# Forming the turns of an S5 layer earlier: where sixteen angle and sine blocks stand in a fused two-layer kernel

## The reference, cut to what matters

```python
q_dn, kv_dn, k_rope, gate = jnp.split(h @ w_in, MLA_SPLITS, axis=-1)
```

```python
lam_dt = lam * dt[:, None]
powers = jnp.exp(lam_dt[None] * jnp.arange(1, S5_CHUNK + 1, dtype=jnp.float32)[:, None, None])
```

## Time and profile before

| | us |
|---|---|
| median of three executions | 1883.57 |
| lowest and highest | 1883.27, 1885.47 |
| profiled execution, its own time | 1888.0 |
| its span in the trace | 1886.2 |

### The profile page before, as it was taken

How to read it: one execution, slowest core, us unless ns; L and a number is a source line. 1 busy time by engine, 2 the same in 40 slices (tenths; PEclk the granted TensorE clock), 3 DMA queues, 4 the chain that set the end, 5 groups by cost and what they waited for, 6 DMA issues and landing times.

```text
span 1886.2 us, 27230 instructions
## 1 busy us (share of the span) xinstructions
PE 1646.9 (87%) x10616; PEld 1230.7 (65%) x10616; DVE 659.5 (35%) x1225; ACT 409.9 (22%) x922; POOL 661.3 (35%) x678
## 2 busy tenths in 40 slices
PE   3899659999999959999566699999989998999997
PEld 3444225555554438888455588888878786888786
DVE  4565936565550042230666600001023012233301
ACT  1303333323220020001544410000021001244300
POOL 0026999999899999600333200000000000000000
PEclk9999879999999989999877799999999999999999
DMA  8669878788788866326898854444423432344431
GB/s 268 192 200 250 219 167 173 173 184 205 195 193 194 192 139 148 111 67 228 253 300 280 239 160 148 154 156 133 156 77 125 134 112 67 121 148 154 150 124 61
DMA packets 241230, 318.31 MB, mean 169 GB/s; under 512 B 32274, under 2 KB 211061, under 8 KB 236405
## 3 DMA queue, kind: packets, MB, share of 16 engines
q1 hardware_dynamic: 204736, 227.58, 37.8%
q0 software_dynamic: 33072, 80.79, 20.1%
q10 hardware_dynamic: 3333, 8.71, 1.4%
HBM read 258.28 MB, written 50.33 MB: 164 GB/s over the span
## 4 chain that ended last, share of the span: by engine, by line
PE 75%; DVE 8%; DMA 5%; ACT 4%; issue 4%; SPq 3%; DVEq 0%; ACTq 0%; PEldq 0%
PE bank L830 34%; PE bank L1143 12%; PE bank L1028 6%; DMA arena<-s_b_powers 3%; PE bank L897 2%; SPq L646 2%; DMA s_turns<-arena 2%; PE bank L854 2%; PE bank L1083 1%; PE bank L1199 1%; PE bank L961 1%; PE bank L930 1%; PE bank L929 1%; PE bank L927 1%; PE bank L928 1%
## 5 line engine op out<-in xcount | busy, mean ns | idle before, releaser
L830 PE MATMUL bank<-ht,ring 128*128 128x256 f32 (+1 forms) x1664 | 425.9, 419 | 27.0 <-ACT gate L1344 16.4
L830 PEld LDWEIGHTS bank<-ht,ring 128*128 128x128 f32 x1664 | 321.9, 194 | 128.8 <-issue 89.3
L1143 PE MATMUL bank<-arena,ring 128*128 128x256 f32 x1024 | 223.2, 381 | 1.0 <-PEq L1134 1.0
L1143 PEld LDWEIGHTS bank<-arena,ring 128*128 128x128 f32 x1024 | 195.9, 191 | 28.1 <-issue 1.2
L830 PE MATMUL bank<-gate,ring 128*128 128x256 f32 (+1 forms) x640 | 195.0, 467 | 4.9 <-DVE gate L2176 3.4
L830 PEld LDWEIGHTS bank<-gate,ring 128*128 128x128 f32 x640 | 122.6, 192 | 76.8 <-issue 63.1
L1028 PE MATMUL bank<-ring,ht 128*128 128x256 f32 x512 | 116.5, 391 | 17.4 <-DVE ht L1777 17.4
L1028 PEld LDWEIGHTS bank<-ring,ht 128*128 128x128 f32 x512 | 100.5, 197 | 32.1 <-issue 17.8
L830 PE MATMUL bank<-arena,ring 128*128 128x256 f32 x480 | 108.0, 388 | 3.9 <-DVE arena L2238 3.9
L830 PEld LDWEIGHTS bank<-arena,ring 128*128 128x128 f32 x480 | 93.8, 196 | 17.9 <-DVE arena L2238 4.3
L2375 POOL DMA_DIRECT2D arena<-arena x128 | 64.7, 513 | 109.9 <-ACT arena L1505 108.0
(11 more groups left out here) (362 smaller groups left out, 2349.4 us busy)
## 6 DMA issues: line engine op xcount, KB each, us to landing
ring<-in_s_w_glu SPq DMA_DIRECT2D x32, 1024.0 KB, 5.3
ring<-in_w_mod SPq DMA_DIRECT2D x24, 1024.0 KB, 9.1
ring<-in_w_up SPq DMA_DIRECT2D x22, 1024.0 KB, 5.1
arena<-s_b_rows POOLq DMA_DIRECT2D x32, 512.0 KB, 11.6
arena<-s_power_rows POOLq DMA_DIRECT2D x32, 512.0 KB, 11.6
s_b_powers<-arena POOLq DMA_DIRECT2D x32, 512.0 KB, 3.1
s_c_powers<-arena POOLq DMA_DIRECT2D x32, 512.0 KB, 5.6
ring<-in_s_w_in SPq DMA_DIRECT2D x16, 1024.0 KB, 5.5
```

Source lines behind the costliest of these rows:

```text
L830: mm = pe.matmul(psum[2 * (u % 2) + m][:, 0:mv.free_size()], ring[:, sl, k, m * P:(m + 1) * P], mv, start=(kg == 0 and k == 0), stop=(kg = ...
L1143: mm = pe.matmul(psum[4 * par + 2 * (s // 2) + m][:, 0:S], ring[:, sl, k, m * P:(m + 1) * P], yt[:, kg * 8 + k, :], start=(kg == 0 and k = ...
```

## The change

Six of the sixteen blocks (0 to 5) are formed during the MLA head, angle and sines both. Angles 0 and 1 stand on DVE ahead of the copies of `qd`, angles 2 to 5 behind them, and ACT takes the six blocks ahead of its squares. Two more output buffers are laid over free room at the start of the arena, so the first four blocks have a buffer each; blocks 4 and 5 go back to the first two and wait for stores. Angles 6 to 9 are also formed there, and kept in four extra buffers in the same room, so DVE first waits until all six stores have landed. ACT may write the second half of `b_and_c` (that is `ccol`, which lies over the angle and output buffers) only after angle 9 is formed and the six stores have landed. The other blocks stand behind gate units 2 (6, 7, 8), 3 (9, 10, 11), 4 (12, 13) and 5 (14, 15). DVE forms angles 10 to 15 ahead of the normalisation of queries and keys, and none behind it. The wait of ACT for `bc_spilled` moves from unit 4 to unit 2. No operation is added or taken away.

```diff
+        trig_angle += [carve(512 * i, 2, BLK, NC5) for i in range(4)]
+        trig_out += [carve(1024 * i, 2, 2, BLK, NC5) for i in range(2)]
+        def angle_of(b):
+            return trig_angle[b - 4 if 6 <= b < 10 else b % 2]
+        def trig_of(b):
+            return trig_out[b if b < 4 else b % 2]
...
             def b_and_c():
                 for f in range(16):
+                    if f == 8:
+                        act.wait_ge(ang_set, 10)
+                        for par in range(2):
+                            act.wait_ge(trig_stored[par], 16 * 3)
...
             modulate(0)
+            def trig(b):
+                par = b % 2
+                angle, o = angle_of(b), trig_of(b)
+                act.wait_ge(ang_set, b + 1)
+                if b >= 4:
+                    act.wait_ge(trig_stored[par], 16 * (b // 2))
...
+            for b in range(6):
+                trig(b)
...
-            trigs = ((), (), (0, 1, 2), (3, 4, 5), (6, 7, 8, 9), (10, 11, 12, 13), (14, 15), ())
+            trigs = ((), (), (6, 7, 8), (9, 10, 11), (12, 13), (14, 15), (), ())
             for s in range(8):
                 if s == 4:
...
-                    act.wait_ge(bc_spilled, 8 * 16)
-                gate_silu(s)
+                gate_silu(s)
+                if s == 2:
+                    act.wait_ge(bc_spilled, 8 * 16)
...
+            def angles(b):
+                angle = angle_of(b)
+                if 2 <= b < 6 or b >= 10:
+                    dve.wait_ge(trig_set, 2 * (b - 6 if b in (10, 11) else b - 2) + 2)
...
+            for b in range(2):
+                angles(b)
             dve.wait_ge(par_got, 6)
...
+            for b in range(2, 6):
+                angles(b)
             dve.wait_ge(slot_done, at + 2)
...
+            for par in range(2):
+                dve.wait_ge(trig_stored[par], 16 * 3)
+            for b in range(6, 10):
+                angles(b)
...
-            for b in range(6):
+            for b in range(10, NB5):
                 angles(b)
             dve.wait_ge(root_set, 2)
...
-            for b in range(6, NB5):
-                angles(b)
```

More of the change, by code:

```diff
@@ L1332, in _ @@
             modulate(0)
+            def trig(b):
[4 more added lines that the diff above has]
+                    act.wait_ge(trig_stored[par], 16 * (b // 2))
+                act.activation(o[:, 1], angle, ACT.Sin, scale=-TWO_PI_DOWN).then_inc(trig_set, 1)
+                link(act.activation(o[:, 0], angle, ACT.Abs))
+                act.activation(o[:, 0], o[:, 0], ACT.Sin, scale=-TWO_PI_DOWN, bias=half_pi).then_inc(trig_set, 1)
+                act.wait_ge(trig_set, 2 * b + 2)
+                act.dma_start(spill_trig[b], o.rearrange("p z d q c -> p (z d q c)")).then_inc(trig_stored[par], 16)
+            for b in range(6):
+                trig(b)
             for j in range(2):
@@ L1345, in gate_silu @@
                         .then_inc(unit_free[(u0 + s) % 2], 1)
-            def trig(b):
-                par = b % 2
-                act.wait_ge(ang_set, b + 1)
-                if b >= 2:
-                    act.wait_ge(trig_stored[par], 16 * (b // 2))
-                act.activation(trig_out[par][:, 1], trig_angle[par], ACT.Sin, scale=-TWO_PI_DOWN).then_inc(trig_set, 1)
-                link(act.activation(trig_out[par][:, 0], trig_angle[par], ACT.Abs))
-                act.activation(trig_out[par][:, 0], trig_out[par][:, 0], ACT.Sin, scale=-TWO_PI_DOWN, bias=half_pi)\
-                    .then_inc(trig_set, 1)
-                act.wait_ge(trig_set, 2 * b + 2)
-                act.dma_start(spill_trig[b], trig_out[par].rearrange("p z d q c -> p (z d q c)")).then_inc(trig_stored[par], 16)
-            trigs = ((), (), (0, 1, 2), (3, 4, 5), (6, 7, 8, 9), (10, 11, 12, 13), (14, 15), ())
+            trigs = ((), (), (6, 7, 8), (9, 10, 11), (12, 13), (14, 15), (), ())
             for s in range(8):
@@ L1819, in _ @@
                 dve.tensor_copy(pw[:, z, :, GP5:P], pn[:, z, ::-1, GP5:P]).then_inc(par_got, 1)
+            def angles(b):
+                angle = angle_of(b)
+                if 2 <= b < 6 or b >= 10:
+                    dve.wait_ge(trig_set, 2 * (b - 6 if b in (10, 11) else b - 2) + 2)
+                ph = phi[:, :].rearrange("p (d q) -> p d q", d=2)[:, :, b * BLK:(b + 1) * BLK].unsqueeze(3).to_broadcast(wide)
+                link(tt(angle, ph, iota.unsqueeze(1).unsqueeze(1).to_broadcast(wide), ALU.mult))
+                link(ts(trig_near, angle, MAGIC, None, ALU.add))
+                stt(out=angle, in0=trig_near, scalar=-MAGIC, in1=angle, op0=ALU.add, op1=ALU.subtract).then_inc(ang_set, 1)
+                dve.wait_ge(ang_set, b + 1)
+            for b in range(2):
+                angles(b)
             dve.wait_ge(par_got, 6)
@@ L1863, in _ @@
             dve.wait_ge(bc_spilled, 8 * 16)
-            def angles(b):
-                par = b % 2
-                if b >= 2:
-                    dve.wait_ge(trig_set, 2 * b - 2)
-                ph = phi[:, :].rearrange("p (d q) -> p d q", d=2)[:, :, b * BLK:(b + 1) * BLK].unsqueeze(3).to_broadcast(wide)
-                link(tt(trig_angle[par], ph, iota.unsqueeze(1).unsqueeze(1).to_broadcast(wide), ALU.mult))
-                link(ts(trig_near, trig_angle[par], MAGIC, None, ALU.add))
-                stt(out=trig_angle[par], in0=trig_near, scalar=-MAGIC, in1=trig_angle[par], op0=ALU.add, op1=ALU.subtract)\
-                    .then_inc(ang_set, 1)
-                dve.wait_ge(ang_set, b + 1)
-            for b in range(6):
+            for b in range(10, NB5):
                 angles(b)
```

## The result

| kernel | median us (lowest to highest, executions) | ratio to before, 95% |
|---|---|---|
| before | 1883.42 (1881.20 to 1885.47, 4) | |
| changed | 1853.45 (1852.55 to 1855.85, 4) | 0.9836 (0.9811 to 0.9862) |
| changed, second time | 1854.56 (1851.23 to 1858.36, 4) | 0.9849 (0.9827 to 0.9871) |
| changed, third time | 1853.54 (1849.20 to 1857.27, 4) | 0.9837 (0.9814 to 0.9859) |

The change makes the kernel 30.0 us faster, where 36.8 was forecast. The time lies in the range (1842 to 1859) and 6.7 us above the forecast of 1846.8. The changed kernel's profiled execution took 1855.85 us, with a span of 1854.0 where before had 1886.2.

What follows compares the result with a forecast made beforehand. PE was taken to bound the kernel, with two waits for ACT totalling 38.9 us. Heads 34.8 us earlier, net of a 5.7 us head delay, plus 1.95 for their first products gave 36.8 us, so 1846.8 us; range 1842 to 1859.

Steps and rivals of the forecast that it cites:

- Both gaps: PE's waits for ACT around gate unit 7, 16.4 us before it and 22.5 before the heads; both would go.
- third rival: Gate units: silu 4 comes out behind 191.9 and PE waits again, 2 to 8 us each, 1849 to 1855; 5%.
- POOL's tables (fourth): S5 layer: POOL's tables bind its start and the kernel is slower, 1889 us or up to 1905; 3%.
- the normalisation (first): Before the heads: DVE's normalisation, behind angle 15, becomes last; 0 to 8 us, 1847 to 1855; upper part 20%.
- the forecast's own upper bound without rivals: Whole kernel: 1851 us, if the two store landings in the head sum to 13 us.
- A: Head: landing time of the store of block 2, which block 4 waits for; taken as 3.5 us.
- B: Head: landing time of the store of block 5, which DVE waits for beside a 1 MB gate load; 5 us.
- A + B - 2.8: Head: delay of the second half of `b_and_c` from two store landings; 5.7 us, bounds 2.4 to 21.2.
- The clock was charged at nothing: Head: PE's clock stays full if PE goes on with turning pieces; no charge, otherwise about 2 to 3 us.
- 221.2: Start of the heads in us, instead of 256.02, with both gaps gone and unit 7 at full clock; 34.8 us saved.
- Against the median, to which the same saving applies: Whole kernel: the 36.8 us summed from the profiled execution also come off the median 1883.57, giving 1846.8.
- Nothing else of the later stages changes: Behind the heads: the 36.8 us stand to the end; POOL's table slack falls from 89.4 to 46.9 us.

Runs made afterwards that it cites:

- head only: Changed kernel with blocks 6 to 15 back where they stood before, six blocks and ten angles still in the head; 1879.44 us (0.9973), again 1877.74 (0.9966).
- The pause: Kernel without store waits in the head, plus POOL holding half of table 12 until DVE wrote the layer norm's output; 1842.91 us against 1847.17 without.
- spread only: Kernel before with its sixteen blocks spread later over gate units 2 to 7, nothing moved to the head; median 1882.04 us (0.9985).

## Why the prediction was right, and where its size was off

**Right.** Both gaps went, and nearly by the mechanism put: silu 4 was out at 183.4 where 186 was worked out and 191.9 was the limit, silu 5 waited for PE, and units 4 to 7 ran unbroken. The heads' first eight products took 3.70 us where 3.45 was put. POOL's first table started at 164.84, forecast 165. The wait in the gate units (third rival) did not come back, POOL's tables (fourth) did not bind, and the normalisation (first) was not last: its angles ended at 194.5 where 198.5 was put. In the second trace it ended only 6.7 us before PE wanted it, and head only shows that this rival was no fancy. The median of 1853.45 us lies above 1851, the forecast's own upper bound without rivals, though the landings stayed within the 13 us for which that bound stood; the range held because it was widened for the rivals.

**Half of a cause was misread.** The prediction says that ACT is late because of its own blocks of sines. The timeline of ACT before shows, between silus 4 and 5:

```profile
195.82 0.63 ACT L1353 ACTIVATE arena<-arena 128x512 f32<-128x512 f32 x1 [16.70 <-DVE arena L1872]
...
209.70 0.63 ACT L1353 ACTIVATE arena<-arena 128x512 f32<-128x512 f32 x1 [8.32 <-DVE arena L1872]
```

Of the 36.0 us from the end of silu 4 to silu 5, ACT spent 28.0 waiting for DVE's angles, which were formed behind the normalisation and beside POOL's scalings. The change cures this too, because it forms the angles first. The sum did not depend on the misreading, since it charged both gaps whole.

**The landings in the head were mis-sized.** I took A = 3.5 and B = 5 us; they were 5.74 and 6.19. The formula A + B - 2.8 gives 9.1, less 0.8 because store 2 was issued at 72.92 and not at 73.7: 8.3, and 8.16 was measured. The formula held and its terms did not. For A I had read an idle DMA row of before; but the change itself fills it, with four stores issued between 67.6 and 75.2. The six stores of the head, from issue to landing:

```profile
DMA to landing us min/median/max: 3.0/5.6/7.5
```

The hold of 8.16 us is 2.5 over my 5.7. For B I had 5 us if the queues take turns and 8 if the load is served first. The Trainium skill ("DMA: Bandwidth & Descriptors", section "Queues, rings and completion order") says that each DMA engine takes turns between the queues; the 6.19 lies nearer to that estimate. The 3.03 of the store that was issued ahead of its load shows that the order of issue matters as much.

**The clock was charged at nothing.** I wrote that PE would go on with pieces of the turning. Stretches of the changed kernel (us, busy us of PE, PEld, DVE, ACT, POOL, clock, DMA share, GB/s):

```profile
96.00:100.00 4.00, 1.04 (x5) 1.04 (x6) 3.90 (x4) 3.02 (x4) 0.00 (x0) 0.70 0.00 0
100.00:104.00 4.00, 4.00 (x15) 2.93 (x14) 3.93 (x3) 4.00 (x5) 0.00 (x0) 0.50 0.00 0
104.00:108.00 4.00, 4.00 (x10) 1.65 (x9) 3.97 (x2) 0.25 (x1) 0.00 (x0) 0.95 0.00 0
```

After an idle time of 5.63 us and 16 short products the granted clock was at half, 1.2 instead of 2.4 GHz, as unit 0 began, and 28.59 - 27.70 = 0.9 us went there. In the other two traces of the changed kernel, after 5.0 and 4.9 us, the row lost 0.4 and 0.1, and head only lost nothing in this row after 5.4 in its second trace; so the term is 0 to 0.9 us. In the kernels that start the copies within 4 us of before, that row took 27.70 or 27.71. In the first trace hold and clock together put the heads 3.1 us behind 221.2, and the first products took 0.25 more than put: 3.4 of the missing 6.8. In the other two the heads were 2.7 and 0.7 us behind.

**The saving was read from one execution.** "Against the median, to which the same saving applies" is a step that no row supported. That trace was 4.4 us over its median, and though it took only 1.9 us more than the second trace in all, it was 3.2 us longer in the very stretch that was summed. A mean of the two would have forecast 1.6 us less.

**"Nothing else of the later stages changes" was wrong for the layer norm.** It took 39.8 to 40.0 us in three traces of the changed kernel, 38.3 and 37.1 in two of before: 2.2 us by the means. The eight modulations and the two products `xc` and `xl` with `arena` (L2026, L2004 before) took DVE 12.7 and 11.9 us in the two traces of before, and 14.7, 14.0 and 13.9 in the three of the changed kernel, which is 1.9 of the 2.2. The pause shows that these operations lengthen by what POOL does beside them. That the changed kernel meets more of POOL's products because its heads end earlier is inferred from that, and was not isolated.

3.4, 1.6 and 2.2 make 7.2, and 6.8 is missing, but the account closes better than its parts allow. The traces of the changed kernel end 34.3 us before those of before by the means, where the medians say 30.0. What the sum leaves out is the S5 input, which was 4.8 us shorter by the same means, and it scatters: it took 184.3 us in one trace of the changed kernel and 188.3 in another. Its row of the first, and of the second trace:

```profile
675.00:863.00 188.00, 180.22 (x832) 156.97 (x832) 35.34 (x73) 17.66 (x38) 105.65 (x97) 0.97 0.56 160
```

```profile
676.00:860.00 184.00, 176.16 (x832) 153.93 (x832) 35.52 (x73) 17.53 (x38) 105.91 (x97) 0.99 0.57 164
```

The same 832 matmuls cost 4 us more at a clock of 0.97 than at 0.99. Both traces of before show 190, spread only shows 184.4, and since it changes nothing there either, I count this stretch to scatter; two traces of before don't settle that. For the same reason head only remains partly open: its heads are 17 us earlier than before and its layer norm gives 6 back, but its medians are only 5 and 6.5 us better; its loop to the end, 994.5 and 992.6 us, is among the longest in the table, and nothing here explains it.

## What to carry to other kernels

A DMA row that is idle before the change says nothing of the transfers that the change puts there: count the change's own stores in it, and look at whether each is issued ahead of or behind a large load. Take a saving that is summed from waits from more than one execution. When an engine is late, look at what it waits for before you blame its own work. And of two parts of a change, each of little worth alone, ask what each frees for the other; here the blocks in the head pay only if ACT then hands DVE its buffers early.

## What the runs showed of the hardware

- A half-megabyte store took 3.03 us when issued 0.84 us ahead of a load of 1 MB, and 6.19 when issued 1.40 behind such a load. Over eleven traces the first case gave 3.0 to 3.6 us, and over seven of them the second gave 5.5 to 6.2.
- DVE's operations from and to SBUF lengthened by what POOL did beside them, small ones most: eight of 128x256 took 2.8 us with POOL silent and 6.2 to 9.9 beside its products of 1.3 us, one of 128x2048 took 2.3 and up to 3.6, and one of 0.42 us took 3.90 beside a scaling of 5.41. Making POOL wait, where it has slack, was worth 4.3 us by the medians.
- The first two gate units took 27.70 us at full clock. In six traces with a wait of 4.9 to 5.6 us just ahead of them the granted clock was at half shortly before they began, and they lost 0 to 0.9 us. After 15.4 and 16.4 us without work unit 7 took 15.63 and 16.73 us, where half of two units at full clock is 13.8.
